# Hybrid decoder trunk: the gate and up products of the ConvGLU as seven block products

## The reference, cut to what matters

```python
D_MODEL, SEQ, DEPTH = 1024, 1024, 2
D_FF = ((8 * D_MODEL // 3 + 127) // 128) * 128          # 2816: 22 tiles of 128

def conv_glu_ffn(h, w_up, conv_w, w_down):
    gu = h @ w_up                                       # gates and ups, 2 x 2816 columns
    g, u = jnp.split(gu, 2, axis=-1)
    g = causal_dwconv(g, conv_w)                        # 3 taps over positions
    return (jax.nn.silu(g) * u) @ w_down

def reference(...):
    h = x
    for layer in range(DEPTH):
        h = h + hybrid_mixer(rms_norm(h, norm_mix_g[layer]), ...)
        h = h + conv_glu_ffn(rms_norm(h, norm_ffn_g[layer]), w_up[layer], conv_ffn_w[layer], w_down[layer])
    return rms_norm(h, final_g)
```

## Time and profile before

| what | value |
|---|---|
| median of 3 runs | 2656.47 us (2655.26 to 2659.01) |
| the profiled execution | 2659.75 us, span 2657.9 us |
| PE busy | 2526.0 us, 95% of the span |
| DVE, ACT, POOL busy | 61%, 24%, 30% |
| granted PE clock, mean | 0.978 of full |
| the three passes L451 to L453 in the chain that ended last | 24%, 23%, 23% |

### The profile page before, as it was taken

How to read it: one execution, slowest core, us unless ns; L and a number is a source line. 1 busy time by engine, 2 the same in 40 slices (tenths; PEclk the granted TensorE clock), 3 DMA queues, 4 the chain that set the end, 5 groups by cost and what they waited for, 6 DMA issues and landing times.

```text
span 2657.9 us, 29833 instructions
## 1 busy us (share of the span) xinstructions
PE 2526.0 (95%) x12006; PEld 2106.5 (79%) x12006; DVE 1615.5 (61%) x2113; ACT 631.0 (24%) x1229; POOL 790.5 (30%) x434
## 2 busy tenths in 40 slices
PE   8799999899999999999979999979999999999996
PEld 6688887777888888888868888868778888888885
DVE  8544677536655566666774456773466666666665
ACT  3344444431000001100313344442210000011002
POOL 3112122242333333333321122131523333333332
PEclk9899999899999999999989999989999999999998
DMA  3000000211111111111210000111111111111111
GB/s 138 24 25 25 33 32 24 82 48 40 51 53 48 48 48 48 48 48 49 93 57 24 25 32 25 32 62 45 56 48 48 48 48 48 48 48 48 48 50 70
DMA packets 52761, 127.34 MB, mean 48 GB/s; under 512 B 4624, under 2 KB 22160, under 8 KB 52624
## 3 DMA queue, kind: packets, MB, share of 16 engines
q1 hardware_dynamic: 51040, 124.14, 14.0%
q10 hardware_dynamic: 1584, 1.28, 0.2%
HBM read 116.76 MB, written 8.39 MB: 47 GB/s over the span
## 4 chain that ended last, share of the span: by engine, by line
PE 82%; DVE 12%; ACT 2%; issue 2%; POOL 1%; DMA 0%; DVEq 0%; POOLq 0%
PE ps L451 24%; PE ps L453 23%; PE ps L452 23%; PE ps L624 3%; PE ps L611 2%; DVE h L1031 2%; PE ps L598 1%; PE ps L599 1%; ACT prob L843 1%; DVE h L1029 1%; DVE q_next L1006 1%; PE ps L571 1%; DVE prob L1065 1%; PE ps L561 1%; DVE k_next L1229 1%
## 5 line engine op out<-in xcount | busy, mean ns | idle before, releaser
L451 PE MATMUL ps<-x_hi,w_hi 128*128 128x512 f32 x2304 | 914.8, 397 | 7.9 <-issue 6.0
L453 PE MATMUL ps<-x_hi,w_lo 128*128 128x512 f32 x2304 | 901.8, 391 | 0.0
L452 PE MATMUL ps<-x_lo,w_hi 128*128 128x512 f32 x2304 | 901.1, 391 | 0.0
L377 POOL CAST w_hi<-stage 128x1024 fp32r<-128x1024 f32 (+1 forms) x198 | 207.6, 1048 | 1787.7 <-PE ps L453 1711.7
L379 POOL TENSOR_TENSOR w_lo<-stage,w_hi 128x1024 fp32r<-128x1024 f32 (+1 forms) x198 | 524.5, 2649 | 15.9
L451 PEld LDWEIGHTS ps<-x_hi,w_hi 128*128 128x128 f32 x2304 | 435.8, 189 | 99.2 <-issue 10.1
L453 PEld LDWEIGHTS ps<-x_hi,w_lo 128*128 128x128 f32 x2304 | 435.0, 189 | 92.8
L452 PEld LDWEIGHTS ps<-x_lo,w_hi 128*128 128x128 f32 x2304 | 435.6, 189 | 89.7 <-issue 1.9
L969 DVE TENSOR_TENSOR h<-ps,h 128x1024 f32<-128x1024 f32 x320 | 391.4, 1225 | 64.7 <-PE ps L453 28.3
L1229 DVE SCALAR_TENSOR_TENSOR k_next<-padded,vec,k_next 128x1024 f32<-128x1024 f32 x88 | 178.1, 2024 | 57.8 <-ACT k_next L902 56.2
L949 DVE TENSOR_TENSOR q_next<-ps,rstd_all 128x512 f32<-128x512 f32 x112 | 77.0, 690 | 208.6 <-PE ps L453 191.1
(11 more groups left out here) (155 smaller groups left out, 2638.0 us busy)
## 6 DMA issues: line engine op xcount, KB each, us to landing
stage<-stream SPq DMA_DIRECT2D x180, 512.0 KB, 3.2
h<-x_t SPq DMA_DIRECT2D x16, 512.0 KB, 5.5
stage<-stream SPq DMA_DIRECT2D x16, 448.0 KB, 4.5
saved_h<-h SPq DMA_DIRECT2D x8, 512.0 KB, 4.7
h<-saved_h SPq DMA_DIRECT2D x8, 512.0 KB, 3.4
out_t<-h SPq DMA_DIRECT2D x16, 256.0 KB, 2.1
stage<-stream SPq DMA_DIRECT2D x16, 64.0 KB, 4.7
dilated_mask<-dilation ACTq DMA_DIRECT2D x1, 512.0 KB, 9.0
```

The source lines that it names most:

```text
L377: pool.tensor_copy(w_hi[:, s, wide], stage[:, s, wide]).then_inc(pool_seq, 1)
L451: pe.matmul(out, w_hi[:, s, w], hi, start=start, stop=False)
L452: pe.matmul(out, w_hi[:, s, w], lo, start=False, stop=False)
L453: return pe.matmul(out, w_lo[:, s, w], hi, start=False, stop=stop)
```

## The change

Let A be a hidden tile's weights as a 2x2 of blocks: rows by halves of the 1024 input features, columns gate (1) and up (2); B is the normed x as a 2x2: rows halves of the features (k), columns halves of the positions (t). The four results (gate and up, t = 0 and 1) were eight block products of 12 matmuls; they are now seven (Strassen's scheme in Winograd's form). The blocks `S1` to `S4` are sums of weight blocks, `T1` to `T4` of x blocks.

- The x blocks (B11, B21, B22, T1 to T4, each hi and lo) are made once a layer, in `first_blocks`, from x that is already normed, and lie in SBUF room that attention uses otherwise. So the cos and sin tables and the masks are loaded again for layer 1 (`load_tables`), and cos and sin are saved to DRAM once.
- Weights come as half tiles ("blocks") of 128x512; there are four rooms for them in `w_hi` and `w_lo`. A room is free when the product, or down group, four blocks before is done. POOL forms S1 to S4 in the staging slots (four now) and subtracts; ACT rounds, apart from the first 11 blocks of a layer, which POOL rounds.
- For each hidden tile DVE joins the seven products (`combine`), seven additions of 512 columns, the fifth of which frees the bank of the seventh product. `value` follows behind the convolution and the last addition.
- The down projection takes two hidden tiles at a time: both go into the same PSUM bank, so each row tile is added once for a pair. It uses two pairs of banks instead of three, and stands behind the products of the next tile but one (`feed_forward`).
- In the output projection the last halves come in the order `LATE_ORDER`, so that the norm of t = 0 goes beside the last two.
- The order of first products (`FIRST`) is another than that of later ones (`STEADY`).

The third column of `STEADY` and `FIRST` is the PSUM bank. P1 to P7 are a tile's products in the order in which they run.

```diff
+PAIRS = F_TILES // 2
+ADDS = (PAIRS - 1) * KT + 2 * KT
...
+STEADY = (("A11", "B11", 0), ("A22", "T4", 1), ("S1", "T1", 2), ("S2", "T2", 3), ("S3", "T3", 0), ("A12", "B21", 3),
+          ("S4", "B22", 2))
+FIRST = (("A11", "B11", 0), ("A12", "B21", 1), ("S4", "B22", 4), ("S3", "T3", 5), ("S2", "T2", 0), ("S1", "T1", 1),
+         ("A22", "T4", 6))
+PRODUCTS = len(STEADY)
...
+LATE_ORDER = ((5, 0), (5, 1), (6, 0), (7, 0), (6, 1), (7, 1))
...
+def feed_forward():
+    work = [("up", 0), ("up", 1)]
+    for pair in range(PAIRS - 1):
+        work += [("up", 2 * pair + 2), ("down", pair), ("up", 2 * pair + 3)]
+    return work + [("down", PAIRS - 1)]
...
+    for what, n in feed_forward():
+        if what == "up":
+            for _ in range(PRODUCTS):
+                products += 1
+                blocks.append(("products", products))
+        else:
+            for _ in range(2):
+                downs += KT // 2
+                blocks += [("downs", downs)] * 2
...
+            def first_weights():
+                (a11, a12), (a21, a22) = staged(), staged()
+                whole_block(a11)
+                whole_block(a12)
+                s3 = a11
+                combine(s3, a11, a21, ALU.subtract)
+                s4 = a12
+                combine(s4, a12, a22, ALU.subtract)
+                combine(s4, s4, s3, ALU.add)
+                whole_block(s4)
+                whole_block(s3)
+                s2 = a11
+                combine(s2, a22, s3, ALU.subtract)
+                whole_block(s2)
+                s1 = a21
+                combine(s1, a21, a22, ALU.add)
+                whole_block(s1)
+                whole_block(a22)
+                pool.sem_inc(stage_free, 2)
+            def weights(rounded):
+                (a11, a12), (a21, a22) = staged(), staged()
+                s1, s2, s3, s4 = a22, a11, a21, a12
+                if rounded:
+                    whole_block(a11)
+                    whole_block(a22)
+                else:
+                    pool.sem_inc(block_raw, 2)
+                    rest_of_block(a11)
+                    rest_of_block(a22)
+                combine(s1, a21, a22, ALU.add)
+                if not rounded:
+                    pool.sem_inc(block_raw, 1)
+                combine(s3, a11, a21, ALU.subtract)
+                combine(s2, s1, a11, ALU.subtract)
+                if rounded:
+                    whole_block(s1)
+                    whole_block(s2)
+                    pool.sem_inc(block_raw, 2)
+                else:
+                    pool.sem_inc(block_raw, 3)
+                    rest_of_block(s1)
+                    rest_of_block(s2)
+                rest_of_block(s3)
+                rest_of_block(a12)
+                combine(s4, a12, s2, ALU.subtract)
+                pool.sem_inc(block_raw, 1)
+                rest_of_block(s4)
+                pool.sem_inc(stage_free, 2)
...
+            def block_pass(out, n, w, hi, lo, start, stop):
+                columns = slice(w * P, (w + 1) * P)
+                pe.matmul(out, block_of(w_hi, n)[:, columns], hi, start=start, stop=False)
+                pe.matmul(out, block_of(w_hi, n)[:, columns], lo, start=False, stop=False)
+                return pe.matmul(out, block_of(w_lo, n)[:, columns], hi, start=False, stop=stop)
+            def product(x, b, between={}, fresh=False):
+                n = next_block()
+                pe.wait_ge(block_ready, n + 1)
+                hi, lo = x_blocks[x]
+                for k in range(KT // 2):
+                    if k in between:
+                        between[k]()
+                    if fresh:
+                        pe.wait_ge(x_hi_ready, seen(x_hi_ready))
+                        pe.wait_ge(x_lo_ready, seen(x_lo_ready))
+                    ended = block_pass(bank(b), n, k, hi[:, k, :], lo[:, k, :], k == 0, k == KT // 2 - 1)
+                ended.then_inc(product_done, 1)
...
+                    earlier = {"B11": 3 - PRODUCTS, "T4": 4 - PRODUCTS, "T1": 0, "T2": 6 - PRODUCTS, "B21": 1, "B22": 5}
+                for _, x, b in STEADY:
+                    if x == "T3":
+                        pe.wait_ge(first_kept, layer * F_TILES + f + 1)
+                    elif x in earlier:
+                        pe.wait_ge(combined, before + earlier[x])
+                    product(x, b)
...
+            def down(layer, pair):
+                blocks = [next_block() for _ in range(4)]
                 for m in range(KT):
-                    pair = m % DOWN_PAIRS
-                    if pair in pair_held:
-                        pe.wait_ge(add_done, pair_held[pair] + 1)
+                    if m % (KT // 2) == 0:
+                        here = blocks[m // (KT // 2) * 2:][:2]
+                        pe.wait_ge(block_ready, here[1] + 1)
...
+                        pe.wait_ge(add_done, layer * ADDS + pair * KT + m - 1)
                     for t in range(2):
-                        ended = three_pass(bank(DOWN + 2 * pair + t), s, slice(m * P, (m + 1) * P),
-                                           mix_hi[f % 2][:, halves_of_t[t]], mix_lo[f % 2][:, halves_of_t[t]], True, True)
+                        for f in range(2):
+                            ended = block_pass(bank(DOWN + 2 * (m % 2) + t), here[f], m % (KT // 2),
...
+            def round_blocks(count):
+                for _ in range(count):
+                    layer, n = divmod(block_at[0], blocks_of_layer)
+                    at = block_at[0]
+                    block_at[0] += 1
+                    act.wait_ge(block_raw, seen(block_raw))
+                    wait_used(act, layer, n - W_BLOCKS)
+                    act.activation(block_of(w_hi, at), raw_block(layer, n), ACT.Copy).then_inc(block_hi, 1)
...
+                round_blocks(1)
+                if follows:
+                    silu()
+                keep_first(layer, f)
+                round_blocks(1)
+                if follows:
+                    keep_value(f - 1)
+                round_blocks(3)
+                center(layer, f)
+                round_blocks(2)
...
+            def first_blocks(layer):
+                norm, rows = 2 * layer + 1, range(KT // 2)
+                def take(x, k):
+                    m, t = {"B11": (k, 0), "B21": (KT // 2 + k, 0), "B12": (k, 1), "B22": (KT // 2 + k, 1)}[x]
+                    dve.scalar_tensor_tensor(x_raw[x][:, k, :], h[:, m, halves_of_t[t]], gain_of(layer, V_FFN_G, m),
+                                             bank(NORM[t]), ALU.mult, ALU.mult).then_inc(xn_ready, 1)
+                def form(x, k, a, b, op):
+                    dve.wait_ge(xn_ready, max(made(layer, a, k), made(layer, b, k)))
+                    dve.tensor_tensor(x_raw[x][:, k, :], x_raw[a][:, k, :], x_raw[b][:, k, :], op).then_inc(xn_ready, 1)
+                def rest(x, k):
+                    dve.wait_ge(x_hi_ready, seen(x_hi_ready))
+                    hi, lo = x_blocks[x]
+                    dve.tensor_tensor(lo[:, k, :], x_raw[x][:, k, :], hi[:, k, :].bitcast(f32), ALU.subtract)\
+                       .then_inc(x_lo_ready, 1)
+                dve.wait_ge(spread_done, 2 * norm + 1)
+                for k in rows:
+                    take("B11", k)
+                    if k == 1:
+                        partial(norm, 1, SUMMED_FFN)
+                for k in rows:
+                    rest("B11", k)
+                take("B21", 0)
+                take("B21", 1)
+                roots(1)
+                take("B21", 2)
+                take("B21", 3)
+                for k in rows:
+                    rest("B21", k)
+                add_product(layer, 0, 2, padded[:, TAPS - 1:TAPS - 1 + HALF], 1, q_next[:, 0:HALF], first_kept)
+                dve.wait_ge(spread_done, 2 * norm + 2)
+                for k in rows:
+                    take("B22", k)
+                for k in rows:
+                    rest("B22", k)
+                    take("B12", k)
+                for k in rows:
+                    form("T3", k, "B22", "B12", ALU.subtract)
+                for k in rows:
+                    rest("T3", k)
+                    dve.wait_ge(x_lo_ready, rested(layer, "B11", k))
+                    form("T2", k, "T3", "B11", ALU.add)
+                for k in rows:
+                    rest("T2", k)
+                    dve.wait_ge(x_lo_ready, rested(layer, "B22", k))
+                    form("T1", k, "B22", "T2", ALU.subtract)
+                for k in rows:
+                    rest("T1", k)
+                    dve.wait_ge(x_lo_ready, rested(layer, "B21", k))
+                    form("T4", k, "T2", "B21", ALU.subtract)
...
+            def combine(layer, f):
+                gates, ups = padded[:, TAPS - 1:], q_next[:, :]
+                low_gates, high_gates, low_ups, high_ups = gates[:, 0:HALF], gates[:, HALF:], ups[:, 0:HALF], ups[:, HALF:]
+                u2, u3 = low_gates, high_gates
+                add_product(layer, f, 4, low_ups, 3, u2, first_kept)
```

(41 more changed lines are left out.)

573 lines of the change are left out of this document (383 added, 190 removed).

## The result

The changed kernel takes 2672.5 us (median of 5 runs, 2670.6 to 2674.8) against 2656.8 for the kernel before in the same job: ratio 1.006, 95% interval 1.0047 to 1.0072. It is slower by 0.6% where 0.4% faster was forecast. The profiled execution took 2670.58 us, its span 2668.6 (before: 2659.75 and 2657.9).

The account below looks back on a forecast made before the run. PE, busy 95% of the span, was taken as the bound. Terms -118.9 + 80 + 22 + 6 = -11 us against the profiled 2659.75 gave 2649, or 2646 as median of runs; 8-in-10 range 2600 to 2692.

Parts of the forecast that it names:

- 528 matmuls less: Feed-forward hidden tiles: 12 fewer matmuls in each of 22 tiles, 2 layers, at 0.2252 us each: -118.9 us.
- first tiles: First tile of each layer: PE waits while DVE makes x blocks, 62.9 us per layer; +80 us in all.
- value chain ahead of down: Down pairs: PE waits 1.1 us for the first add_down before the third group, 20 times; +22 us.
- end of a layer: Before last_down, which waits for four down blocks at once: 3.4 us in place of 0.3; +6 us in all.
- 7 lost today: Start of each feed-forward in the kernel before: 5.6 us of PE waits plus some 1.5 us of slow clock.
- They alternate: First tile: DVE two-SBUF-operand and POOL instructions take turns, each POOL one delaying DVE by its length; 12 us taken.
- Clock: First tile: cold clock on the last blocks of P2 and P7 and tile 1's start, 3 us together (0 to 5).
- Ordinary tiles: Tiles after the first: no stall on weight blocks, and P7's wait for five adds 0.3 us from one.
- rival D: Weight blocks late in ordinary tiles, 2 to 3 us a pair, +40 to 60: 2695 us; chance 0.08.
- A: Likeliest case, the whole kernel with the terms as summed: 2646 us, own range 2628 to 2666; chance 0.50.
- C: Slower: port alternation in full at first tile (49 a layer) and value chain (46), end 8: 2690 us; chance 0.17.
- B: POOL and DVE hardly meet: first tile 50.9 us, no stall ahead of down, 2596 us; chance 0.25.

Follow-up runs that it names:

- 416 bytes: Kernel after with 416 unused bytes ahead of q_split, nothing else changed: 2636.1 us, ratio 0.9921.
- everything lined up: Kernel after with only the SBUF order changed, q_split, k_twice and mix right behind w_lo and the small tensors behind them: 2635.8 us, ratio 0.9916.
- the run with short sums: Lined-up kernel after with the 16 sums of x blocks a layer cut to 4 of 512 columns, so the result is not valid: 2621.8 us, ratio 0.9864.

## Why the prediction was wrong

The terms of the sum, with the kernel after at the pace of before (416 bytes) and as it is, from the starts of matmuls in the three traces:

| term | forecast | pace of before | as it is |
|---|---|---|---|
| 528 matmuls less | -119 | -120 | -120 |
| first tiles | +80 | +73 | +68 |
| value chain ahead of down | +22 | +11 | +1 |
| end of a layer | +6 | +7 | +7 |
| slower matmuls, feed-forward | 0 | 0 | +39 |
| slower matmuls elsewhere | 0 | 0 | +11 |
| the rest elsewhere | 0 | +5 | +5 |
| sum | -11 | -24 | +11 |
| measured, profiled span | | -23.8 | +10.7 |

The +39 counts every product, also those of the first tiles, where PE waits for DVE anyway; so the first tiles lose less at the slow pace.

**The step that failed** is one sentence of the first part: "There a matmul less is 0.2252 us less". It prices what goes, and takes it for granted that the 5808 matmuls that stay in the feed-forward, and the others, keep their price. They lost 6.7 ns each, by a change of address that came with the blocks of x: q_split, mix and x lie 96 bytes off the weights, modulo 256, behind small tensors whose sizes don't sum to a multiple of 256. Nothing in the forecast, neither a term nor a rival, stood for it. With it taken away by 416 bytes the kernel is at 2636.1, inside the likeliest case's own range of 2628 to 2666, and faster as forecast. That it is not far from the 2646 of that case is in part luck, as two of the terms below show.

- *Matmuls removed*: right in count (12006 to 11478). The price of 0.2252, from a count per window, is 0.2267 from start to start.
- *First tile*: 45.3 us lost where 47 were said is luck, for the make was wrong. Tile 0 took 55.9 us where its own sign of being right was 60 to 66, and tiles 1 and 2, put at nothing, lost 9.0. The 12 us put on DVE's list as contention are 5.6: its sets of four rests took 4.64, 3.77 and 4.39 us for an undisturbed 2.49, and one sum 0.3 more. The "7 lost today" is 11.3 a layer: 22 small matmuls of the norm also stood in that stretch of the kernel before, 5 us of PE's time, and they were not in the 7. "They alternate" is false for the cast of 16.67 us. It is true in the same trace a little later, for rests that DVE also issued without a gap, as in the earlier trace rows. First DVE, then POOL:

```profile
649.13 4.39 DVE L1612 TENSOR_TENSOR T_lo<-x_first,T_hi 128x512 fp32r<-128x512 f32 x4
...
649.32 0.96 POOL L544 CAST w_hi<-stage 128x512 fp32r<-128x512 f32 x1 [0.34 <-POOL w_lo L552]
650.37 1.60 POOL L552 TENSOR_TENSOR w_lo<-stage,w_hi 128x512 fp32r<-128x512 f32 x1
```

  What decides between the two no run shows. The Trainium skill, page "SBUF — State Buffer", section "Terms", says that the two share a pair of ports which one takes for a whole instruction while the other stands. The 16.67 us cast says more than that: the loser can stand through some 28 instructions in a row (16.67 / 0.60).
- *Clock*: three stretches of the first tile, kernel after (clock third from the end):

```profile
605.00:610.00 5.00, 4.39 (x14) 3.35 (x14) 5.00 (x6) 0.47 (x1) 3.03 (x2) 0.50 0.01 3
...
640.00:645.00 5.00, 3.94 (x14) 1.94 (x12) 5.00 (x9) 2.71 (x5) 5.00 (x1) 1.00 0.00 0
...
650.00:655.00 5.00, 4.94 (x14) 3.19 (x15) 4.82 (x5) 0.00 (x0) 4.49 (x5) 0.66 0.63 210
```

  The first product, behind 6.5 us of wait, ran at 1.2 GHz (0.43 us between starts); with waits of 0.3 to 0.4 us between groups of three matmuls it was at 2.4 GHz, and behind the next wait of 2.4 us at 1.2 again for most of the next 5 us (0.66). So neither all seven products cold nor none. What it cost in tile 0 was not measured by itself; in tiles 1 and 2 the matmuls behind the two waits for POOL cost some 3.6 us, which no term had.
- *Value chain*: the mechanism was right, its size not. Adds at T-3.2, centre 1.16 and convolution 3.52 came as priced, but silu does not wait for the last add. The kernel after, T = 887.86:

```profile
884.82 1.16 ACT L1227 ACTIVATE k_next<-padded,vec 128x1024 f32<-128x1024 f32 x1 [1.30 <-DVEq L1690]
886.01 3.52 DVE L1704 SCALAR_TENSOR_TENSOR k_next<-padded,vec,k_next 128x1024 f32<-128x1024 f32 x2
889.57 0.69 DVE L1676 TENSOR_TENSOR q_next<-ps,q_next 128x512 f32<-128x512 f32 x1
889.63 1.06 ACT L1246 ACTIVATE k_next<-k_next 128x1024 f32<-128x1024 f32 x1 [0.89 <-DVEq L1694]
890.73 1.22 DVE L1711 TENSOR_TENSOR k_next<-k_next,q_next 128x1024 f32<-128x1024 f32 x1 [0.47 <-ACT k_next L1246]
892.10 1.23 DVE L1343 TENSOR_TENSOR h<-ps,h 128x1024 f32<-128x1024 f32 x1
```

  The first add_down ends at 893.33, T+5.5 for the forecast's T+6.5. PE needs it 24 matmuls behind T, which is T+5.6 at 0.2334 and T+5.4 at 0.2267. The slow pace hides the stall; part of its price is paid back here.
- *End of a layer*: 2.9 us of wait, as said; in layer 0 1.6 us are lost inside the last down, 0.6 before. +7 in both layers for +6.
- *Ordinary tiles*: PE waits in none for a block or for the fifth add, the 0.3 us of slack held, rival D did not come.
- *Rivals*: the time lies between A and C, but nothing of C is in it. C's threshold is added up wrongly in the forecast: its 11 us are 6 us a layer or 0.6 us a pair, not both. B's condition, that POOL and DVE hardly meet, was not met.

The row of slower matmuls elsewhere: attention and projections have some 6 ns on each 512-wide product too, but it comes through only where PE is the one that is late; the stretch between the two feed-forwards is 592.3 us after and 586.3 with everything lined up. The 5 us of the rest were not followed further.

## What to carry to other kernels

When a change adds, drops or reorders SBUF tensors, count the matmuls per window, or take start to start, ahead of any other comparison: a busy share of 100% hides a slower pace. Then print the byte addresses, and pad so that weights and moving operand start alike modulo 256; it cost 416 bytes of each partition here and gave 1.4%. Where VectorE and GpSimd meet with operands in SBUF, price both lists together, and look which of the two came late: here GpSimd stood for 16 us beside one run of VectorE and took turns with others, and letting it in first gained nothing.

## What had not been expected of the hardware

- A 128x512 fp32r product with w_hi or w_lo takes 0.2267, 0.2289, 0.2334, 0.2325 to 0.2328 and 0.2333 us for starts that differ by 0, 64, 96, 128 and 192 bytes modulo 256. The start by itself doesn't matter (all moved by 32 bytes: 2657.4), nor which lies lower.
- A GpSimd cast of 0.61 us stood 16.67 us against VectorE instructions with two SBUF operands issued every 0.60 us, and those were not slowed. The same cast took 16.1 to 16.9 us in both layers of every changed kernel with whole sums and no waits for POOL between them.
- In the run with short sums a 128x4 sum takes 0.15 us, or 1.25 where it meets GpSimd, and then it ends with GpSimd's instruction (638.38 and 638.35). First DVE, then POOL:

```profile
637.13 1.25 DVE L1602 TENSOR_TENSOR x_second<-x_second,x_first 128x4 f32<-128x4 f32 x1
...
636.67 1.68 POOL L547 TENSOR_TENSOR w_lo<-stage,w_hi 128x512 fp32r<-128x512 f32 x1
```

  So in that run the two take turns where, with whole sums, GpSimd stood.
